# Two transformer blocks on one core: norm sums by quarters of tokens, context scaled early by GpSimd, attention scores a step ahead

## The chip, the cores and the metric

One core of one Trainium2 chip runs the whole kernel, in float32 results throughout. The metric is device time in microseconds (us) of one execution. PE is TensorE, PEld its weight loads, DVE is VectorE, ACT is ScalarE, POOL is GpSimd, SP is SyncE, which issues the loads.

## The reference, cut to what matters

There are 256 latent tokens and 256 context tokens of width 1024. A first block (state space mixer, pooling, gates, then a routed mixture of 32 experts) is followed by a second one of two layers: feed-forward, mixer, feed-forward; the mixer of layer 0 is gated linear attention beside latent attention, that of layer 1 is a neighbourhood attention. After each part stands a norm over the 1024 features of each token:

```python
def layer_norm_2(x):
    mu = jnp.mean(xf, axis=-1, keepdims=True)
    var = jnp.mean(jnp.square(xf - mu), axis=-1, keepdims=True)
    return ((xf - mu) * lax.rsqrt(var + EPS)).astype(x.dtype)
def modulate_2(x, shift, scale):
    return x * (1.0 + scale) + shift
xl = post_norm_2(xl, 0.5 * g1 * swiglu_2(modulate_2(xl, sh1, sc1), ffn1_w_in[l], ffn1_w_out[l]))
```

Layer norms: after the first block's mixer ("out1", latents, 256 columns) and after its experts ("out2", 256); then after feed-forward 1, mixer and feed-forward 2 of layer 0 and feed-forward 1 of layer 1 (512 columns, latents and context together), and after the mixer and feed-forward 2 of layer 1 (256 columns). RMS norms stand in the first block's gate (over 2048 features), in the gated linear attention (each of 4 heads, 128 features) and in the latent projections (128 and 384 features).

## The kernel before, in words

Activations lie transposed: 128 features on the partitions, tokens along the columns, 8 tiles for 1024 features. A linear layer multiplies with three fp32r products for each pair of tiles: weights and activations are each cut into a high part (ACT copies to fp32r, AH and HR) and a low part (DVE subtracts, AL and LR). Weights come in loads of up to 1 MB through three slots; ACT's and DVE's `take` cut a load two ahead of the one that PE uses. Each engine has its own program in its own order (`tensor_program`, `scalar_program`, `vector_program`, `pool_program`), tied by counting semaphores; all order around the change is written out by hand.

Sums over features are fp32 matmuls with `K.onesD`, a 128x128 matrix of 1/1024, so that every partition gets the sum of its column. `mean_pe` (L567) adds the tile m-1 to the mean after PE's linear tile m, so that seven of eight sums stand among the linear's matmuls, and the last follows the last residual (`residual_dve`). Then `norm_dve` (L625) subtracts the mean from the eight tiles, `norm_act` (L612) squares them, `norm_pe` (L600) sums the squares, ACT takes the root over all columns into `rs`, DVE inverts it there (`V.rec`, L259), and multiplies each tile. ACT scales and shifts a multiplied tile, cuts its high part, DVE its low part (`lead_act`, `lead_dve`), and PE's next linear starts with tile 0. POOL multiplies the residual (`lead_pool`).

```python
    S.wait_ge(*pe.of(tag, "var"))
    S.wait_ge(*act.last)
    S.act(rs, K.ps(tag, "var")[:, 0:n], ACT.Sqrt, bias=K.eps[:, eps:eps + 1]).then_inc(*act(tag, "root"))
```

Between the experts and the first feed-forward, `after_dve` (L2087) adds the residual, cuts eight tiles of the scaled context, cuts two loads of weights and only then centres; `after_act` (L2060) scales the context. The context's tokens are loaded to `K.X` while the experts run (`route_sp`). The gated linear attention ends with one RMS norm per head (`gla_pe` from L2334, `gla_act`, `gla_dve`), and `latent_pe` (L2687), `latent_act`, `latent_dve` begin with two more. In the neighbourhood attention (`odd_pe` L2928, `odd_act`, `odd_dve`) a step is one head and half of the queries, 32 steps. In step n PE issues the scores of n, then in every second step the values of an earlier head, then the transposes of n-2. DVE adds the bias, takes the maximum, and later multiplies by the inverse sum; ACT takes the exponential and copies transposes and values out of PSUM.

PSUM has eight banks in rotation (`Tensor.bank`); during a norm one is held for the mean and one for the variance. The conditioning steps (`conditioning_pe`) are 16 fp32 matmuls of a weight tile 128x32 (`K.CS`) with 128 columns, each to one of four groups of 32 output partitions; the trace counts each fp32 matmul as two instructions.

## Time and profile before

| | us |
|---|---|
| median of 3 runs | 3332.53 (3329.27 to 3336.29) |
| the profiled execution | 3333.78 |
| its span | 3332.0 |
| outside the span | 1.78 |
| PE busy | 3049.1 (92% of the span) |
| DVE busy | 1418.6 (43%) |
| ACT busy | 1079.1 (32%) |
| POOL busy | 308.4 (9%) |
| mean granted TensorE clock | 0.957 of full |

A share of busy time is an average over stages with different limits. A matmul's end is modelled, so its start and the start of the next tell what it takes. The experts ran in the branch "few", in which every expert has at most 64 tokens.

### The profile page before, as it was taken

Reading aid. Unit: us, or ns where it says so; the run is one execution under the profiler, and the core shown is the slowest. Engines: PE = TensorE matmul, PEld = TensorE weight load, DVE = VectorE, ACT = ScalarE, POOL = GpSimd, SP = SyncE. Lnnn points to the kernel's source line nnn. Section 1 sums busy time; section 2 is a strip of 40 time slices with the busy share of each in tenths; the row PEclk is TensorE's granted clock in tenths of the full one; section 3 lists DMA queues with packets and bytes.
Section 4 is the critical chain, followed back from the end, with each engine's and each line's share of the span. In section 5 each row is a group of like instructions: output and inputs, shape, how many; then the busy total and the mean of one; then the engine's idle time right before and its main releaser. Section 6 shows DMA issues by size and latency. Waiting matters only on the chain.

```text
span 3332.0 us, 43660 instructions
## 1 busy us (share of the span) xinstructions
PE 3049.1 (92%) x18814; PEld 2358.7 (71%) x18814; DVE 1418.6 (43%) x2096; ACT 1079.1 (32%) x1579; POOL 308.4 (9%) x309
## 2 busy tenths in 40 slices
PE   6988899789999979999887888999989999897998
PEld 4866699755555548888676546888768887773898
DVE  4654554532222243333576554333353333436554
ACT  4443453322222233222432233322242221434443
POOL 0024470100000000000104001000010000300000
PEclk9988999879999989999999899999999999999999
DMA  7556754489999943232339121333222323310363
GB/s 226 159 188 219 252 162 135 133 335 392 392 389 395 393 158 98 81 112 71 100 114 335 39 76 51 103 94 102 81 78 88 107 81 103 129 62 1 127 188 103
DMA packets 415213, 537.27 MB, mean 161 GB/s; under 512 B 14340, under 2 KB 389924, under 8 KB 390308
## 3 DMA queue, kind: packets, MB, share of 16 engines
q1 hardware_dynamic: 415012, 534.38, 47.0%
q8 instruction: 151, 2.47, 0.3%
q14 instruction: 50, 0.41, 0.0%
HBM read 533.30 MB, written 1.05 MB: 160 GB/s over the span
## 4 chain that ended last, share of the span: by engine, by line
PE 83%; DVE 8%; ACT 4%; DMA 2%; issue 2%; SPq 0%; POOL 0%; DVEq 0%; ACTq 0%; POOLq 0%
PE ps L188 80%; PE ps L187 2%; ACT ar L313 2%; DVE ar L243 2%; DVE LR L243 1%; DMA RAW<-in_ada_w 1%; DVE ar L259 1%; ACT HR L313 1%; PE ps L194 1%; DVE ar L249 0%; DVE ar L253 0%; DMA RAW<-in_w_in 0%; DVE ar L262 0%; ACT AH L313 0%; DVE X L243 0%
## 5 line engine op out<-in xcount | busy, mean ns | idle before, releaser
L188 PE MATMUL ps<-AH,HR 128*128 128x512 f32 (+1 forms) x2552 | 902.4, 354 | 64.1 <-DVE AL L243 40.5
L188 PE MATMUL ps<-AL,HR 128*128 128x512 f32 (+1 forms) x2552 | 888.6, 348 | 0.0
L188 PE MATMUL ps<-AH,LR 128*128 128x512 f32 (+1 forms) x2552 | 887.6, 348 | 0.0
L243 DVE TENSOR_TENSOR LR<-RAW,HR 128x2048 fp32r<-128x2048 f32 (+3 forms) x232 | 485.4, 2094 | 597.8 <-ACT HR L313 595.1
L313 ACT ACTIVATE HR<-RAW 128x2048 fp32r<-128x2048 f32 (+3 forms) x232 | 404.1, 1744 | 736.9 <-PE ps L188 634.9
L188 PEld LDWEIGHTS ps<-AH,HR 128*128 128x128 f32 x2552 | 492.1, 193 | 136.7 <-ACT arf1i L313 20.3
L188 PEld LDWEIGHTS ps<-AL,HR 128*128 128x128 f32 x2552 | 492.3, 193 | 59.8 <-issue 1.9
L188 PEld LDWEIGHTS ps<-AH,LR 128*128 128x128 f32 x2552 | 491.7, 193 | 58.9
L188 PE MATMUL ps<-ar 64*128 64x128 f32 (+9 forms) x1318 | 237.1, 370 | 59.4 <-ACT ar L313 26.8
L249 POOL TENSOR_SCALAR X<-X 128x512 f32<-128x512 f32 (+2 forms) x50 | 83.8, 1700 | 2220.2 <-ACT AH L313 1608.9
L188 PEld LDWEIGHTS ps<-ar 64*128 64x128 f32 (+2 forms) x1318 | 140.5, 189 | 139.1 <-issue 45.6
L253 DVE SCALAR_TENSOR_TENSOR X<-ps,mod,X 128x256 f32<-128x256 f32 x152 | 67.4, 480 | 284.9 <-PE ps L188 284.9
L243 POOL TENSOR_TENSOR ar<-ar 128x384 f32<-128x384 f32 (+5 forms) x138 | 151.9, 1109 | 291.0 <-DVE ar L243 116.3
L313 ACT ACTIVATE ar<-ar 128x384 f32<-128x384 f32 (+7 forms) x208 | 109.4, 557 | 158.8 <-DVE ar L249 53.9
L313 ACT ACTIVATE ar<-ps 128x256 f32<-128x256 f32 (+4 forms) x190 | 89.2, 475 | 203.8 <-PE ps L188 194.9
L188 PE MATMUL ps<-BHf1i,HR 128*128 128x512 f32 x352 | 144.5, 410 | 0.7 <-ACT arf1i L313 0.7
L188 PE MATMUL ps<-RAW,CS 128*32 128x128 f32 x3072 | 125.9, 315 | 16.6 <-DMA RAW<-in_w_ada 9.0
L313 ACT ACTIVATE ar_few<-ps 128x512 f32<-128x512 f32 x64 | 46.9, 733 | 287.4 <-PE ps L188 287.4
L188 PE MATMUL ps<-BHf1i,LR 128*128 128x512 f32 x352 | 139.7, 397 | 0.0
L188 PE MATMUL ps<-BLf1i,HR 128*128 128x512 f32 x352 | 139.6, 396 | 0.0
L188 PE MATMUL ps<-BHf2i,HR 128*128 128x512 f32 (+1 forms) x352 | 122.7, 349 | 1.4 <-DVE arf2i L243 1.4
L188 PE MATMUL ps<-BHf2i,LR 128*128 128x512 f32 (+1 forms) x352 | 119.1, 338 | 0.0
(182 smaller groups left out, 3748.8 us busy)
## 6 DMA issues: line engine op xcount, KB each, us to landing
RAW<-in_ada_w SPq DMA_DIRECT2D x72, 1024.0 KB, 6.4
RAW<-in_f1i SPq DMA_DIRECT2D x44, 1024.0 KB, 5.1
RAW<-in_f2i SPq DMA_DIRECT2D x44, 1024.0 KB, 5.1
RAW<-in_w_in SPq DMA_DIRECT2D x32, 1024.0 KB, 5.5
RAW<-in_w_ada SPq DMA_DIRECT2D x24, 1024.0 KB, 8.0
RAW<-in_w_eu SPq DMA_DIRECT2D x17, 1024.0 KB, 10.0
HF<-in_w_ed SPq DMA_DIRECT2D x17, 1024.0 KB, 7.5
LF<-in_w_eu SPq DMA_DIRECT2D x17, 1024.0 KB, 10.1
```

Source lines behind the costliest of these rows:

```text
L187: return self.e.matmul(o, w, x, start=start, stop=stop, skip_group_check=True)
L188: return self.e.matmul(o, w, x, start=start, stop=stop)
L194: return self.e.transpose(o, a, self.K.ident[sp:sp + q, sp:sp + q])
L243: return self.e.tensor_tensor(o, a, b, op) if self.e else NOTHING
L249: return self.e.tensor_scalar(o, a, s1, None, o1)
L253: return self.e.scalar_tensor_tensor(out=o, in0=a, scalar=s, in1=b, op0=o1, op1=o2) if self.e else NOTHING
L259: return self.e.reciprocal(x, x) if self.e else NOTHING
L313: return self.e.activation(o, a, f, **k) if self.e else NOTHING
```

## The change

A sum goes by quarters of the tokens: four matmuls with a 128x32 matrix of 1/1024, each for a quarter of the columns, each to its own 32 partitions, so that the sums take a quarter of the columns. ACT's and DVE's steps on sums are then on 64 or 128 columns instead of 256 or 512, and four matmuls with a matrix that picks a row spread the result to all partitions and columns in PSUM. The mean now needs this spreading too, with a copy by ACT ahead of it. The same is done for the RMS norms. `meanwhile` puts work between two steps of a norm. `T.bi = 7` lets the rotation go on with bank 0. In the neighbourhood attention PE issues the scores of step n+1 in step n, and ACT's order changes in odd steps. POOL sets the picking matrix `K.pick` (128x4x128) in `setup_pool` by five more fills. `latent_act` takes all four squares first, then both roots; `latent_dve` inverts both (128 columns), and `latent_pe` spreads both ahead of the projections. The diff, cut; the edits for `rs` in the calls of `norm_act` and `norm_dve` are left out.

```diff
+def sums_pe(T, K, b, x, n, first, last):
+    w = n // 4
+    for g in range(4):
+        r = T.mm(b[32 * g:32 * g + 32, 0:w], K.onesD[:, 0:32], x[:, g * w:(g + 1) * w], first, last)
+    return r
+def spread_pe(T, K, b, x, n):
+    w = n // 4
+    for g in range(4):
+        r = T.mm(b[:, g * w:(g + 1) * w], K.pick[:, g, :], x[:, 0:w], True, True)
+    return r
 def norm_pe(T, K, tag, n, sq):
-    vb, held = T.hold(6, tag, "var")
+    mb, held = T.hold(6, tag, "mean")
...
+    T.wait_ge(*act.of(tag, "mean row"))
+    spread_pe(T, K, mb, K.stat, n).then_inc(*pe(tag, "mean"))
+    vb, held = T.hold(7, tag, "var")
...
     for k in range(8):
-        T.wait_ge(*K.act.of(tag, "sq", k))
-        r = T.mm(vb[:, 0:n], K.onesD[:, :], sq[:, k, :], k == 0, k == 7)
+        T.wait_ge(*act.of(tag, "sq", k))
+        r = sums_pe(T, K, vb, sq[:, k, :], n, k == 0, k == 7)
+    r.then_inc(*pe(tag, "var"))
+    rb, held = T.hold(6, tag, "factor")
...
+    T.wait_ge(*dve.of(tag, "factor row"))
+    spread_pe(T, K, rb, K.stat, n).then_inc(*pe(tag, "factor"))
+    T.hi, T.bi = 8, 7
 def norm_act(S, K, tag, x, n, eps, sq, post, meanwhile=None):
+    row = K.stat[:, 0:n // 4]
+    S.wait_ge(*pe.of(tag, "sums"))
+    S.act(row, K.ps(tag, "sums")[:, 0:n // 4], ACT.Copy).then_inc(*act(tag, "mean row"))
+    K.free(act, tag, "sums")
+    if meanwhile:
+        meanwhile()
...
+    S.act(row, K.ps(tag, "var")[:, 0:n // 4], ACT.Sqrt, bias=K.eps[:, eps:eps + 1]).then_inc(*act(tag, "root"))
 def norm_dve(V, K, tag, x, n, pre, post, meanwhile=None):
+    if meanwhile:
+        meanwhile()
     V.wait_ge(*act.of(tag, "root"))
+    V.rec(K.stat[:, 0:n // 4]).then_inc(*dve(tag, "factor row"))
+    V.wait_ge(*pe.of(tag, "factor"))
...
-            V.tt(x[:, k, :], x[:, k, :], rs, MUL).then_inc(*dve(tag, "normed", k))
+            V.tt(x[:, k, :], x[:, k, :], K.ps(tag, "factor")[:, 0:n], MUL).then_inc(*dve(tag, "normed", k))
 def merge_pe(T, K):
...
-        T.mm(ssq[:, 0:256], K.onesD[:, :], o.sq[m % 2], m == 0, m == 15).then_inc(*pe("ssq", m))
+        sums_pe(T, K, ssq, o.sq[m % 2], 256, m == 0, m == 15).then_inc(*pe("ssq", m))
...
+    T.wait_ge(*dve.of("rz row"))
+    spread_pe(T, K, b, K.stat, 256).then_inc(*pe("rz"))
...
...
+    S.wait_ge(*pe.of("rz"))
+    S.act(o.rz, K.ps("rz")[:, 0:256], ACT.Copy).then_inc(*act("rz"))
+def context_pool(G, K):
+    m = K.mod2[0]
+    G.wait_ge(K.loaded["ctx2"], 16)
+    for k in range(8):
+        G.ts(K.route.h32[:, k, :], K.X[:, k, 0:256], m[:, 8 + k, 1:2], m[:, k, 1:2], MUL, ADD).then_inc(K.scaled, 1)
 def few_pool(G, K):
-    pass
+    context_pool(G, K)
 def after_act(S, K):
...
+    S.wait_ge(K.scaled, 8)
+    for k in range(8):
+        S.act(K.AH[:, k * 512:k * 512 + 256], o.h32[:, k, :], ACT.Copy).then_inc(*act("f1i0h", 1, k))
...
-    for k in range(8):
-        half(k, 0, 1, k % 2)
-    S.cut(1)
-    norm_act(S, K, "out2", o.XL, 256, 0, o.h32, o.rs, post)
+    norm_act(S, K, "out2", o.XL, 256, 0, o.sq2, post, lambda: S.cut(0))
 def after_dve(V, K):
...
-    for k in range(8):
-        half(k, 0, 1, k % 2)
-    V.cut(1)
+    def meanwhile():
+        for k in range(4, 8):
+            context(k)
+        V.cut(0)
+    for k in range(4):
+        context(k)
+    norm_dve(V, K, "out2", o.XL, 256, ("ln2g", "ln2b"), latents, meanwhile)
 def gla_pe(T, K):
...
+    def factor(hd):
+        T.wait_ge(*dve.of("ofactor row", hd))
+        spread_pe(T, K, bank("ofactor", hd), o.rss[hd], 512).then_inc(*pe("ofactor", hd))
...
-        T.mm(bank("omean", hd)[:, :], K.onesD[:, :], o.sqs[hd % 2], True, True).then_inc(*pe("omean", hd))
+        sums_pe(T, K, bank("omean", hd), o.sqs[hd % 2], 512, True, True).then_inc(*pe("omean", hd))
...
+        if hd:
+            factor(hd - 1)
+    factor(3)
 def gla_dve(V, K):
...
+    def onorm(hd):
+        V.wait_ge(*pe.of("ofactor", hd))
+        then(V.stt(o.oT[:, hd, :], o.oT[:, hd, :], K.v("gng"), K.ps("ofactor", hd)[:, :], MUL, MUL))
+        then(V.tt(o.oT[:, hd, :], o.oT[:, hd, :], o.r[:, hd, :], MUL))
...
-        then(V.rec(rs))
+        V.rec(o.rss[hd]).then_inc(*dve("ofactor row", hd))
...
+        if hd:
+            onorm(hd - 1)
+    onorm(3)
 def odd_pe(T, K):
...
+    scores(0)
     for n in range(36):
-        if n < 32:
-            hd, qt = n // 2, n % 2
-            p, m = 64 * (hd % 2), hd // 2
-            T.mm(bank("nsc", n)[:, :], o.qT[p:p + 64, m, qt * 128:qt * 128 + 128], o.kT[p:p + 64, m, :], True,
-                 True).then_inc(*pe("nsc", n))
+        if n < 31:
+            scores(n + 1)
 def odd_act(S, K):
...
     for n in range(36):
+        if n % 2 and 2 <= n < 34:
+            turned(n - 2)
         if n < 32:
+            share(n)
...
+        if n % 2 == 0 and 2 <= n < 34:
+            turned(n - 2)
```

## Rows read from the trace of the kernel before

**Rows 1.** The page: chain that ended last, by engine.
```profile
PE 83%; DVE 8%; ACT 4%; DMA 2%; issue 2%; SPq 0%; POOL 0%; DVEq 0%; ACTq 0%; POOLq 0%
```

**Rows 2.** Chain of waits after the first FFN: start us, us, what.
```profile
1616.83 1.14 PE ps L188 x2
...
1619.40 7.15 PE ps L188 x16
...
1626.57 0.70 ACT arf1i L313
...
1634.03 11.14 PE ps L188 x38
```

**Rows 3.** Timeline there: start, us, engine, line, op [idle before].
```profile
1599.94 1.02 PE L188 MATMUL ps<-X,onesD 128*128 128x512 f32 x2
...
1601.03 0.39 PE L188 MATMUL ps<-BLf1i,HR 128*128 128x512 f32 x1
...
1623.60 1.28 ACT L313 ACT_TABLE_LOAD   x1
```

**Rows 4.** Timeline, PE, a conditioning step among fp32r matmuls.
```profile
112.97 1.08 PE L188 MATMUL ps<-RAW,CS 128*32 128x128 f32 x32
...
114.33 0.40 PE L188 MATMUL ps<-AL,HR 128*128 128x512 f32 x1
114.57 0.40 PE L188 MATMUL ps<-AH,LR 128*128 128x512 f32 x1
```

**Rows 5.** Groups of DVE by form: reciprocals.
```profile
L259 DVE RECIPROCAL ar<-ar 128x512 f32<-128x512 f32 x11 | 36.9, 3353 | 16.3 <-ACT ar L313 16.1
...
L259 DVE RECIPROCAL ar<-ar 128x256 f32<-128x256 f32 x4 | 7.0, 1752 | 11.6 <-ACT ar L313 11.6
```

**Rows 6.** Groups of ACT by form: PSUM to SBUF, 128 columns.
```profile
L313 ACT ACTIVATE mrow<-ps 128x128 f32<-128x128 f32 x96 | 26.2, 273 | 112.7 <-PE ps L188 95.6 <-DMA X<-in_ctxT 16.9
```

**Rows 7.** Timeline, PE: latent projections; full 128x128 weights, 128 columns.
```profile
1906.09 1.91 PE L188 MATMUL ps<-ar,RAW 128*128 128x512 f32 x2
...
1909.88 1.05 PE L188 MATMUL ps<-RAW,ar 128*128 128x128 f32 x8
1910.77 1.02 PE L188 MATMUL ps<-ar,RAW 128*128 128x512 f32 x2
```

**Rows 8.** Windows: width, PE, PEld, DVE, ACT, POOL busy, granted clock, DMA.
```profile
1628.00:1630.00 2.00, 0.00 (x0) 0.00 (x0) 2.00 (x1) 0.00 (x0) 0.00 (x0) 0.64 0.00 0
...
1638.00:1640.00 2.00, 2.00 (x9) 1.60 (x8) 2.00 (x4) 1.97 (x5) 2.00 (x2) 0.80 0.00 0
```

**Rows 9.** Chain of waits, the last norm (256 columns).
```profile
3318.29 3.73 PE ps L188 x16
...
3324.34 0.43 DVE X L243
```

**Rows 10.** Timeline, DVE, POOL and PE, between the experts and the first FFN.
```profile
1219.10 0.75 DVE L243 TENSOR_TENSOR AL<-tmp,AH 128x256 fp32r<-128x256 f32 x2
...
1231.60 2.73 DVE L243 TENSOR_TENSOR X<-X,ps 128x256 f32<-128x256 f32 x8
...
1242.33 11.67 POOL L249 TENSOR_SCALAR X<-X 128x512 f32<-128x512 f32 x8 [572.20 <-DVE X L243]
...
1243.57 0.77 PE L188 MATMUL ps<-AH,HR 128*128 128x512 f32 x1 [5.60 <-DVE AL L243]
```

**Rows 11.** Chain of waits, end of the gated linear attention.
```profile
1884.07 0.69 ACT ar L313
...
1894.58 0.64 ACT ar L313
```

**Rows 12.** Waits in the neighbourhood attention: us in total, times, longest.
```profile
DVE ar L243 <- PE ps L188: 17.1, 9, 3.5
...
DVE AL L243 <- ACT AH L313: 14.5, 7, 3.2
```

**Rows 13.** Windows: eight steps of that attention.
```profile
2985.83:3013.32 27.49, 21.02 (x81) 9.76 (x81) 18.64 (x51) 13.17 (x30) 0.00 (x0) 1.00 0.00 0
```

More of the change, by code:

```diff
@@ L564, in row_ready @@
     return lambda k: [K.act.of(tag, "hi", k), K.dve.of(tag, "lo", k)]
+def sums_pe(T, K, b, x, n, first, last):
[8 more added lines that the diff above has]
+    return r
 def mean_pe(T, K, tag, x, n, bank=7):
     T.hi = 7
-    mb, held = T.hold(bank, tag, "mean")
+    mb, held = T.hold(bank, tag, "sums")
     for h in held:
@@ L575, in add @@
         T.wait_ge(*K.dve.of(tag, "x", m))
-        r = T.mm(mb[:, 0:n], K.onesD[:, :], x[:, m, :], m == 0, m == 7)
+        r = sums_pe(T, K, mb, x[:, m, :], n, m == 0, m == 7)
         if m == 7:
-            r.then_inc(*K.pe(tag, "mean"))
+            r.then_inc(*K.pe(tag, "sums"))
     def after(m):
@@ L617, in norm_act @@
     S.wait_ge(*pe.of(tag, "var"))
-    S.wait_ge(*act.last)
-    S.act(rs, K.ps(tag, "var")[:, 0:n], ACT.Sqrt, bias=K.eps[:, eps:eps + 1]).then_inc(*act(tag, "root"))
+    S.act(row, K.ps(tag, "var")[:, 0:n // 4], ACT.Sqrt, bias=K.eps[:, eps:eps + 1]).then_inc(*act(tag, "root"))
     K.free(act, tag, "var")
@@ L765, in setup_pool @@
 def setup_pool(G, K):
-    for t, v in ((K.onesD[:, :], 1.0 / 1024), (K.ones[:, :], 1.0), (K.eps[:, 0:1], 1e-5), (K.eps[:, 1:2], 1e-6)):
+    for t, v in ((K.onesD[:, :], 1.0 / 1024), (K.ones[:, :], 1.0), (K.eps[:, 0:1], 1e-5), (K.eps[:, 1:2], 1e-6),
+                 (K.pick[:, :, :], 0.0)):
         G.fill(t, v).then_inc(*K.pool("constants"))
+    G.wait_ge(*K.pool.last)
+    for g in range(4):
+        G.fill(K.pick[32 * g:32 * g + 1, g, :], 1.0).then_inc(*K.pool("constants"))
+        G.wait_ge(*K.pool.last)
 def setup_act(S, K):
@@ L1214, in merge_pe @@
     pe.note("h1 read")
+    b, held = T.bank("rz")
+    for w in held:
+        T.wait_ge(*w)
+    T.wait_ge(*dve.of("rz row"))
+    spread_pe(T, K, b, K.stat, 256).then_inc(*pe("rz"))
     linear_pe(T, K, "ya", "w_branch_a", None, 16, 0, 8, o.yv, 256,
@@ L1257, in merge_act @@
     S.wait_ge(*pe.of("ssq", 15))
-    S.act(o.rz, K.ps("ssq")[:, 0:256], ACT.Sqrt, bias=K.eps[:, 0:1], scale=0.5).then_inc(*act("rz"))
+    S.act(K.stat[:, 0:64], K.ps("ssq")[:, 0:64], ACT.Sqrt, bias=K.eps[:, 0:1], scale=0.5).then_inc(*act("rz root"))
     K.free(act, "ssq")
@@ L1298, in merge_dve @@
         V.tt(o.xsL[:, m, :], o.xsL[:, m, :], o.sil[m % 2], MUL).then_inc(*dve("yz", m))
-    V.wait_ge(*act.of("rz"))
-    V.rec(o.rz).then_inc(*dve("rz"))
+    V.wait_ge(*act.of("rz root"))
+    V.rec(K.stat[:, 0:64]).then_inc(*dve("rz row"))
     for m in tiles(V, 8, 16):
@@ L2041, in few_pool @@
 def few_pool(G, K):
-    pass
+    context_pool(G, K)
 def after_pe(T, K):
@@ L2700, in latent_pe, with factor @@
             T.wait_ge(*act.of("csq", i, m))
-            T.mm(b[:, :], K.onesD[:, :], o.P[1], m == 0, m == nt - 1).then_inc(*pe("cmean", i, m))
+            r = sums_pe(T, K, b, o.v2[:, i + m, :], 512, m == 0, m == nt - 1)
+        r.then_inc(*pe("cmean", i))
+    def factor(i):
+        b = bank("cfactor", i)
+        T.wait_ge(*dve.of("cfactor row", i))
+        spread_pe(T, K, b, o.P[0][:, 128 * i:128 * i + 128], 512).then_inc(*pe("cfactor", i))
+    factor(0)
+    factor(1)
     j, w = T.weights("ukv", None, 0, 1, 0, 1024, False)
@@ L2762, in latent_act @@
     meet(S, K, "gla end")
[L2763 to L2764 removed]
+    for i, (x, nt) in enumerate(((o.ck, 1), (o.cq, 3))):
         for m in range(nt):
[L2766 to L2773 removed]
+            S.act(o.v2[:, i + m, :], x[:, m, :], ACT.Square).then_inc(*act("csq", i, m))
+    for i, w in enumerate((8.0, 1024.0 / 384)):
+        S.wait_ge(*pe.of("cmean", i))
+        S.act(o.P[0][:, 128 * i:128 * i + 128], K.ps("cmean", i)[:, 0:128], ACT.Sqrt, bias=K.eps[:, 1:2],
+              scale=w).then_inc(*act("croot", i))
         K.free(act, "cmean", i)
@@ L2829, in then @@
         V.wait_ge(*dve.last)
+    for i in range(2):
+        V.wait_ge(*act.of("croot", i))
+        then(V.rec(o.P[0][:, 128 * i:128 * i + 128]), "cfactor row", i)
     for i, (x, nt, key) in enumerate(((o.ck, 1, "kvng"), (o.cq, 3, "qng"))):
-        V.wait_ge(*act.of("croot", i))
-        then(V.rec(o.P[0]))
+        V.wait_ge(*pe.of("cfactor", i))
         for m in range(nt):
-            then(V.stt(x[:, m, :], x[:, m, :], K.v(key, m), o.P[0], MUL, MUL), "cnorm", i)
+            then(V.stt(x[:, m, :], x[:, m, :], K.v(key, m), K.ps("cfactor", i)[:, :], MUL, MUL), "cnorm", i)
+        K.free(dve, "cfactor", i)
     V.take()
```

142 lines of the change are left out of this document (71 added, 71 removed).

## The prediction

> **What bounds the kernel now.** I read the page first: PE holds 83% of the chain that ended last, DVE and ACT 12% [rows 1]. So a change can pay in two ways: fewer columns in a stretch where PE never waits, or a shorter handover where PE does. I then took the chain and the timeline of one norm with 512 columns [rows 2, 3], a conditioning step, which is the same instruction shape as the new sums [rows 4], groups for the durations of small operations [rows 5, 6, 7], the granted clock [rows 8], and the places that the change touches by itself: the last norm [rows 9], the stage before the first feed-forward [rows 10], the end of the gated linear attention [rows 11], the neighbourhood attention [rows 12, 13]. The sum is made against the profiled execution (3333.78 us, span 3332.0 and 1.78 outside it); the median is 1.25 lower. A difference under 0.2%, 6.7 us, I count as none.
>
> **Sums inside the linears.** Two fp32 instructions with onesD and 512 columns start at 1599.94, and the second product behind them at 1601.03; less one product of 0.24 the sum takes 0.85 [rows 3, 4]. Four sets of four quarter matmuls with 128 columns start at 112.97, and the second product behind them at 114.33: 1.12 for four sets and the change back to full weights [rows 4]. With r for a set and c for the change of shape, 4r + c = 1.12: a lone set costs r + c, 0.28 if c is 0, 0.66 if c is 0.5. I take 0.36 (c = 0.1), because neither step of the row stands out. A sum with 256 columns is half of 0.85, 0.43; its set has half the columns and the same instructions; bounds 0.15 and 0.5, and I take 0.30. In each linear six sums are wholly inside PE's stream (the seventh ends while DVE does the last residual): 4 norms x 6 x 0.49 = 11.8, 3 x 6 x 0.13 = 2.3. The 16 sums over z give 2.1, of which I count 1.1 since PE has small waits there; the spreading and the copy of rz (0.9 + 0.4) stand between the last gate and the first product with yv, and cost about 0.8. **-14.4.**
>
> The row shows that a group in the quartered shape takes 1.0 us for 16 matmuls, about a quarter of 16 x 0.22, which full matmuls with as many columns take [rows 7]. Beside it the Trainium skill (TensorEngine Tiling (Array Packing), Key Properties) says that changing the tiling mode, not just the tile, drains TensorE. By that rule c would be paid at each of the 24 + 34 lone sums; at c = 0.5 the 58 sums would give back 0.3 each, 17 us, and the time would be 3295; the row's 1.12 for four sets with one change leaves room for that, but not for more.
>
> **The norm with 512 columns, four times.** Now, from the last residual to PE's next linear (1616.83 to 1634.03) it is 17.2 [rows 2]. Term by term:
> - Mean: before, 1.14 + 0.03. Now the last set 0.5 with its tail, ACT's copy of 128 columns 0.27 [rows 6], the spreading. Four full matmuls with 128 columns take 1910.77 - 1909.88 = 0.89 [rows 7], and 0.2 for the tail; 1.1. With four handovers 2.0. **+0.8.**
> - Squares to root: PE's squares are slower than ACT's: ACT is through at 1623.5, PE at 1626.55 [rows 2, 3]. With sets of 0.36 PE keeps up, and ACT's table load comes due, 1.28 from 1623.60 [rows 3]: the root starts at 1624.9 instead of 1626.57. **-1.7.**
> - Root on 128 columns: nearest is the copy, 0.27; with a bias 0.37 against 0.70. **-0.3.**
> - Reciprocal: 3.35 for 512 and 1.75 for 256, that is 6.25 ns a column and 0.15 fixed, so 0.95 for 128 [rows 5]. **-2.4.**
> - Spreading the factor, new: 1.1 at full clock. But PE has been idle some 2.3 us by then; in this stage the granted clock fell from 1.0 to 0.5 within 4 us after PE's last matmul, and was back at 1638 to 1640, 4 to 6 us after it started [rows 8]. At half clock it is 2.0. I take **+1.5**.
> DVE's multiplication from PSUM costs what it did (0.7), and ACT's scaling paces the next tiles as before. A norm gains 2.1 (bounds 1.1 and 3.0): **-8.4** for four.
>
> **The norm with 256 columns, three times** (out1, nout, the last). Mean +1.1 (the same number of instructions, full weights). PE's squares end at 3322.0 [rows 9], with ACT's table load just before it: -0.1. Root -0.25. Reciprocal 0.55 against 1.75: -1.2. Spreading +1.1 to +2.0. Net +0.65 to +1.55, so **+3.3** for three: these lose on the handover and win it back in the stream.
>
> **Before the first feed-forward.** DVE cuts the context from 1219.10, then two loads of weights, and centres only from 1231.60; PE starts at 1243.57 [rows 10]. Now GpSimd, idle for 572 us before 1242.33 [rows 10], scales the context while the experts run: eight operations with half the columns of those at 1242.33, under 1.5 us each, hidden by PE's work on the experts; without that cover they would cost up to 12. DVE's work ahead of centring is four subtractions (1.4), to 1220.6, and the spread mean is there at 1220.9: centring starts 10.7 earlier. Squares, table load and root are through at 1226.3, but DVE has four subtractions and one cut of weights (2.3) between, to 1227.2; reciprocal and spreading to 1228.8, and PE at 1232.0: -11.6. The second load is cut later now: ACT waits for POOL's last multiplication (11.67 long, from 1230.8), cuts it by 1244.4, DVE by 1246.8; PE wants it at 1245.9. +0.9. **-10.7** (bounds -7 and -13).
>
> **Gated linear attention and latents.** The last head's roots and reciprocals are 1884.07 to 1894.58 [rows 11]: reciprocal, two steps, twice over. With reciprocals of 0.95 and the spreading of head n under the norm of head n-1, DVE is done at 1890.0: -4.5. Then four squares in a row (2.3) in place of four rounds with PE, both roots, both reciprocals, two spreadings at half clock, one norm: PE's projections start at about 1897 instead of 1906.09 [rows 7], -9.0, and run longer at half clock, 4 us where it was 1.7: +1.2. **-7.8** (bounds -5 and -10).
>
> **Scores a step ahead.** Eight steps take 27.49 us, 3.44 each; DVE is busy 2.33 of it and PE 2.63 [rows 13]. DVE stands 17.1 us over all steps for the scores, which PE issues behind values and transposes [rows 12]; with the scores of n+1 issued a step early, that wait goes. Next late is the low part of every second pair, for which DVE waits on ACT (14.5 now [rows 12]); ACT is in turn behind an exponential. Following DVE, ACT and PE in their new orders through four steps gives 9.7 of DVE's work with its handovers and 1.7 of waiting for that low part: 11.4 where it is 13.74 now, 2.34 x 8 = 18.7. I take the smaller, the wait itself: **-17** (bounds: 0 if the other wait takes its place, -26 if PE's 2.63 a step binds alone).
>
> **At nothing.** The five fills at the start end long before the first weights have landed. Beginning with bank 0 only keeps PE off banks 6 and 7: the factor's bank is read until the eighth tile is multiplied, some 12 us, and the rotation comes to it later; without it PE would wait that long.
>
> **Sum.** -14.4 - 8.4 + 3.3 - 10.7 - 7.8 - 17 = -55.0: 3333.8 becomes 3278.8, and by the median 3277.5.
>
> **Rivals.**
> - The attention gains little, because the low part's wait takes over: 3277.5 + 15 = 3292.5. For it: that wait is nearly as long. Against: in its new order ACT reaches the values no later. Chance 0.13.
> - It gains more: DVE's own work binds the attention, PE's clock stays full through shorter gaps (0.9 less at each spreading): 3277.5 - 9 - 7 = 3261.5. Chance 0.10.
> - Slower: a quarter sum by itself, between full matmuls, does not run its four parts side by side, as they do in a row of sixteen, and pays for both changes of shape. Then a set takes 8 x 0.11 and about 0.3, 1.2. Against the forecast the linears lose 24 x 0.84 = 20 (512 columns) and 34 x 0.9 = 31 (256); the squares wait for PE again, 8 x 1.2 = 9.6 where the table load leaves 5.5 and 3.6: 4 x 4.1 + 4 x 6.0 = 40. The time is 3277.5 + 91 = 3368; it decides from a set of about 0.9, where the 55 us are used up. Against: 1.12 for sixteen matmuls [rows 4]. Chance 0.04. (It is the drain of the page above, at its worst.)
> - The clock stays at half after each sparser norm for so long that it takes the rest: 55 us lost are 110 us at half clock. Against: 4 to 6 us per norm now [rows 8]. Part of it gives a time within 0.2% of before, chance 0.02.
>
> **How the numbers follow.** The forecast has 0.71, and 3277.5 is its time; the bounds of its terms, taken as independent, are 12 us to either side. For 8 in 10 the range reaches to the times of the first two rivals and a little past them: 3257 to 3297. Faster: 0.94; the same: 0.02; slower: 0.04.
>
> **What would show it.** 128x32 matmuls on X in the linears at 0.3 to 0.4 a set; PE's gap after the first feed-forward near 15 us; the reciprocal of 128 columns at 0.95; centring of out2 near 1221 on the old scale; DVE's wait for scores near zero, and the 32 steps in about 93 us instead of 110. I am wrong if a lone set takes over 0.8, if the attention's pair of steps stays at 6.9, or if the clock after a norm stays at 0.5 for over 8 us.

## The result and the profile after

The changed kernel takes **3296.49 us** (median of 4 runs, 3292.12 to 3300.18) where the kernel before took 3331.03 beside it (4 runs, 3329.27 to 3336.29). The ratio is 0.9893, with a 95% interval of 0.9880 to 0.9905: faster by 34.5 us by the medians. The forecast was 55 us faster, 3277.5; the measured time lies half a microsecond inside the upper end of its range (3257 to 3297). The profiled execution took 3299.07 us, with a span of 3297.3.

The page of the changed kernel (busy times, then the chain that ended last by engine; it answers to [rows 1]):

```profile
PE 3044.2 (92%) x19910; PEld 2357.8 (72%) x19910; DVE 1381.8 (42%) x2096; ACT 1072.3 (33%) x1580; POOL 317.3 (10%) x322
...
PE 82%; DVE 8%; ACT 5%; DMA 3%; issue 2%; POOL 1%; SPq 0%; DVEq 0%; ACTq 0%; POOLq 0%
```

PE is busy 5 us less and the span is 35 us shorter, so 30 us of PE's idle time have gone. That doesn't make the gain all waiting: the mean granted clock fell from 0.957 to 0.949, and laid over the clock's records PE's busy time holds 252 us at half clock where it held 201. Counted at full clock PE's work shrank by some 30 us, and half clock took about 26 of it back. To see where the gain came, I cut both traces at the starts of GpSimd's multiplications of the residual, which begin when the first tile of the next linear is ready, right after each norm. The timeline of POOL after (start us, us, line, op):

```profile
1233.93 11.69 POOL L249 TENSOR_SCALAR X<-X 128x512 f32<-128x512 f32 x8 [536.32 <-ACT AH L313]
1621.80 13.45 POOL L249 TENSOR_SCALAR X<-X 128x512 f32<-128x512 f32 x8 [376.18 <-ACT AH L313]
...
2049.11 13.44 POOL L249 TENSOR_SCALAR X<-X 128x512 f32<-128x512 f32 x8 [235.96 <-ACT AH L313]
2434.17 13.44 POOL L249 TENSOR_SCALAR X<-X 128x512 f32<-128x512 f32 x8 [371.62 <-ACT AH L313]
2819.25 13.43 POOL L249 TENSOR_SCALAR X<-X 128x512 f32<-128x512 f32 x8 [371.63 <-ACT AH L313]
...
3085.37 7.58 POOL L249 TENSOR_SCALAR X<-X 128x256 f32<-128x256 f32 x8 [222.25 <-ACT AH L313]
```

| stretch | before, us | after, us | difference | forecast |
|---|---|---|---|---|
| up to the norm before the first FFN | 1242.33 | 1233.93 | -8.4 | -10.7 |
| first FFN and its norm | 391.01 | 387.87 | -3.1 | -5.0 |
| linear attention, latent attention, norm | 433.11 | 427.31 | -5.8 | -12.8 |
| second FFN, norm | 390.74 | 385.06 | -5.7 | -5.0 |
| third FFN, norm | 388.63 | 385.08 | -3.6 | -5.0 |
| neighbourhood attention, norm | 276.36 | 266.12 | -10.2 | -16.7 |
| last FFN, norm, store | 209.82 | 211.93 | +2.1 | +0.3 |

(The forecast column is the terms of the prediction put into their stretches.) All seven have the forecast's sign, and six of them came out worse.

Two rows need care. The first depends on the execution: the join, where the engines' programs meet behind the experts' branch (PE's row `ones,ident` marks it), is at 1215.6 in the trace before, and at 1211.2 and 1210.7 in the traces of experiments 1 and 8, which have the same code up to there. Only what lies behind the join can be read to better than some 5 us: PE's next linear starts 27.95 behind it before (27.8 and 29.2 in experiments 1 and 8) and 20.7 after (20.5 in experiment 7), so -7.2. The second FFN's extra 2 us have no counterpart in the third, which is the same code. In the kernel before PE waits once in the second FFN and not in the third:

```profile
2378.11 0.50 PE L188 MATMUL ps<-BHf2i,HR 128*128 128x512 f32 x1 [1.41 <-DVE arf2i L243]
```

That wait of 1.41 us is in all three traces with the FFN's code of before and in none of the nine with the changed one. Which edit removed it no run shows; no term of the forecast has it.

**A norm with 512 columns.** The chain of waits after the first FFN (start us, us, what), beside [rows 2]:

```profile
1606.58 0.04 issue
1606.63 0.47 PE ps L188 x8
...
1607.12 0.29 ACT stat L313
...
1607.45 1.17 PE ps L188 x8
...
1609.37 4.81 ACT arf1i L313 x8
...
1614.20 1.28 ACT L313
...
1615.49 0.38 ACT stat L313
...
1615.89 0.96 DVE stat L259
...
1616.99 2.06 PE ps L188 x8
...
1622.49 3.75 PE ps L188 x8
```

From the end of the last residual (1606.58) to PE's next linear (1622.49) it is 15.9 where it was 17.2. The mean costs 2.07 up to the centring (1608.65) where it cost 1.21; ACT's root now follows its table load without a wait for PE and starts 8.9 behind the residual instead of 9.8; root and reciprocal are 0.38 and 0.96. What is new is the spreading of the factor: 2.06, at half clock. The granted clock is at half from 1609.5 to 1626.6, 17 us, where before it was from 1628.6 to 1638.8, 10 us: it now falls at the first squares, behind PE's idle time on both sides of the mean's spreading. Most of the longer stretch lies in PE's waits; the next linear has 4.1 us of it (4.8 before).

**A lone sum in the stream**, by PE's timeline there (start us, modelled us), beside [rows 3]:

```profile
1597.70 0.40 PE L188 MATMUL ps<-BHf1i,LR 128*128 128x512 f32 x1
1598.03 0.43 PE L188 MATMUL ps<-X,onesD 128*32 128x128 f32 x8
1598.38 0.50 PE L188 MATMUL ps<-BHf1i,HR 128*128 128x512 f32 x1
1598.72 0.40 PE L188 MATMUL ps<-BLf1i,HR 128*128 128x512 f32 x1
```

Products follow each other by 0.234 us. From the product ahead of the set to the second one behind it there are 1.02 us: 0.55 for the set. The full sum cost 0.85 by the same reading. There is a step of 0.33 ahead of the set and one of 0.34 behind it, each 0.1 more than a product's, as if both changes of shape were to be seen. The change between fp32r products and fp32 sums goes with them, but costs nothing by itself: a full-shape sum between the same products takes 0.85 [rows 3], and one in before's row of squares 0.86 (1620.36 to 1621.22).

**Before the first feed-forward** (timeline of PE, then of DVE; beside [rows 10]; the join, the sums, the start of centring, then the second load of weights):

```profile
1214.47 0.30 PE L188 MATMUL ps<-ones,ident 128*128 128x32 f32 x2
1217.79 1.94 PE L188 MATMUL ps<-X,onesD 128*32 128x64 f32 x64 [3.02 <-DVE X L253]
1220.07 0.48 PE L188 MATMUL ps<-stat,pick 128*128 128x64 f32 x1 [0.34 <-ACT stat L313]
1221.16 1.75 PE L188 MATMUL ps<-stat,pick 128*128 128x64 f32 x7 [0.61 <-issue]
...
1235.17 0.76 PE L188 MATMUL ps<-AH,HR 128*128 128x512 f32 x1 [3.38 <-DVE AL L243]
...
1250.31 0.47 PE L188 MATMUL ps<-AH,HR 128*128 128x512 f32 x1 [1.29 <-DVE LR L243]
```

```profile
1214.81 3.23 DVE L253 SCALAR_TENSOR_TENSOR X<-ps,mod,X 128x256 f32<-128x256 f32 x8 [2.46 <-PE ps L188]
...
1222.95 2.74 DVE L243 TENSOR_TENSOR X<-X,ps 128x256 f32<-128x256 f32 x8 [3.58 <-PE ps L188]
...
1247.87 6.70 DVE L243 TENSOR_TENSOR LR<-RAW,HR 128x2048 fp32r<-128x2048 f32 x3 [3.96 <-ACT HR L313]
```

Centring starts 8.5 us behind the join (16.0 before). PE's sums start 3.0 behind DVE's first residual (1.2 before), and one of the spreading's eight matmuls is followed by 0.61 of "issue", in which PE waits for nothing in the profile. The granted clock is at half from 1217.0 to 1240.9, so the sums, both spreadings and the first 5.7 us of the linear run at half clock. GpSimd's multiplications end at 1245.6, only then do ACT and DVE cut the second load, and PE waits 1.29 for it.

**Neighbourhood attention**: DVE's waits over its steps (us in total, times, longest), beside [rows 12]:

```profile
DVE AL L243 <- ACT AH L313: 10.8, 6, 1.8
DVE ar L243 <- PE ps L188: 8.6, 1, 8.6
DVE ar L243 <- PE ps L194: 8.0, 4, 3.1
```

The wait of 8.6 is the one ahead of the first scores; the kernel before has the same one (8.62, outside the window of [rows 12]). The waits for scores inside the steps went from 17.1 to 8.0, in four places, not to zero; those for the low part from 14.5 to 10.8. Between two low parts (four steps) there are 11.78 us, where there were 13.74 [rows 13]; but the group around 2981 takes 14.4 and two others 12.9. PE's timeline tells the two kinds apart (values and scores of two steps, at full and at half clock; over the two rows themselves the granted clock is 1.00 and 0.51):

```profile
2968.15 2.99 PE L188 MATMUL ps<-ar 64*128 64x512 f32 x10
...
2974.78 5.63 PE L188 MATMUL ps<-ar 64*128 64x512 f32 x10
```

**End of the linear attention and the latents**, chain of waits and PE's timeline, beside [rows 7, 11]:

```profile
1874.74 0.38 ACT ar L313
...
1881.25 2.45 ACT ar L313 x5
```

```profile
1888.40 1.53 PE L188 MATMUL ps<-ar,RAW 128*128 128x512 f32 x2
```

The last head's roots begin 1874.74, ACT's squares of the latents 1881.25, 6.5 us later (10.5 before); PE's projections begin at 1888.40, 13.7 behind the roots' start (22.0 before).

### The profile page after: what moved, and what is told of

Same layout as the page of the kernel before. It is cut to its first block, busy times and chain, and to the rows that moved or that the text cites. A ratio compares the mean times of both kernels' runs of the same rounds, so it can differ in the third digit from the quotient of the medians.

```text
span 3297.3 us, 45861 instructions
## 1 busy us (share of the span) xinstructions
PE 3044.2 (92%) x19910; PEld 2357.8 (72%) x19910; DVE 1381.8 (42%) x2096; ACT 1072.3 (33%) x1580; POOL 317.3 (10%) x322
## 4 chain that ended last, share of the span: by engine, by line
PE 82%; DVE 8%; ACT 5%; DMA 3%; issue 2%; POOL 1%; SPq 0%; DVEq 0%; ACTq 0%; POOLq 0%
PE ps L188 79%; DVE ar L243 2%; PE ps L187 2%; ACT ar L313 2%; DMA RAW<-in_ada_w 1%; DVE LR L243 1%; ACT HR L313 1%; DVE ar L259 1%; DVE ar L249 1%; DMA RAW<-in_w_in 1%; PE ps L194 1%; ACT arf1i L313 1%; DVE ar L262 1%; ACT L313 1%; DVE ar L253 1%
## 5 line engine op out<-in xcount | busy, mean ns | idle before, releaser
L313 ACT ACTIVATE ar<-ps 128x512 f32<-128x512 f32 (+4 forms) x191 | 89.4, 476 | 216.8 <-PE ps L188 194.7
```

Of the source, the lines that this page charges most:

```text
L313: return self.e.activation(o, a, f, **k) if self.e else NOTHING
```

## The experiments

Ten runs were made. Each was timed beside the kernel before; the ratio's interval is 0.1 to 0.2% to either side, 3 to 7 us, so the small effects are read from the stretches of the traces, and the totals only say that they add up.

**1. Scores a step ahead, alone.** The kernel before with the changed loops of the attention on PE and ACT, nothing else:

```diff
+    scores(0)
     for n in range(36):
-        if n < 32:
-            ...
+        if n < 31:
+            scores(n + 1)
```

> The kernel before with one part of the change only: in the neighbourhood attention the scores of step n+1 are issued during step n, and ScalarE takes its copies and exponentials in the new order. Theory A, from the trace after: at full clock four steps take 11.8 us instead of 13.74, six such groups give 11.8, and the stretches at half clock take a part of it back, so the whole kernel is 8 to 12 us shorter (3319 to 3323), with DVE waiting for scores only where the granted clock is below 1. Theory B, the forecast's: -17 (3314) and no such wait left. Theory C: the gain of about 11 in the trace after came from something else before it in time, then under 5 us here.

Measured: 3318.25, ratio 0.9958 (0.9944 to 0.9971), -14 us by the ratio; the stretch of the attention takes 262.68 instead of 276.36, -13.7. DVE's waits in it:

```profile
DVE ar L243 <- PE ps L194: 6.7, 5, 2.1
```

It lies between A and B, nearer to A's mechanism: waits of 1.16 us (four times) and 2.09 remain, each in or right behind a stretch in which the granted clock is at half. The part's gain is real and its own; theory C falls.

**2. Grouped sums.** The changed kernel, with the sums of six tiles in one row:

```diff
     def after(m):
-        if m:
-            add(m - 1)
+        if m == 6:
+            for i in range(6):
+                add(i)
         if m == 7:
+            add(6)
             add(7)
```

> The changed kernel, but the sums of the first six residual tiles are issued in one row behind the seventh tile's products, instead of one set behind each product. Theory A: a lone set costs r + c with c, the two changes of shape, about 0.36 us and r 0.19 (512 columns) or 0.09 (256), since 4r + c = 1.12 and the lone sets of the trace after cost 0.55 and 0.45. Then five changes go in each of seven linears: 7 x 5 x 0.36 = 12.6 us, 3284. Theory B: c is 0.1 as the forecast had it and a lone set costs more for another reason (its wait for DVE's residual, which a group has as well): 3.5 us, 3293. Theory C: the six tiles' sums behind each other make the last tile's products late for DVE: no gain.

Measured: 3277.45, ratio 0.9831 (0.9817 to 0.9845), which is 0.6% below the changed kernel. PE's timeline of one such row:

```profile
1591.11 0.39 PE L188 MATMUL ps<-BHf1i,LR 128*128 128x512 f32 x1
1591.43 1.52 PE L188 MATMUL ps<-X,onesD 128*32 128x128 f32 x48
1592.87 0.50 PE L188 MATMUL ps<-BHf1i,HR 128*128 128x512 f32 x1
1593.21 0.40 PE L188 MATMUL ps<-BLf1i,HR 128*128 128x512 f32 x1
```

1591.11 to 1593.21 is 2.10, less two products 1.63 for six sets: 6r + c = 1.63 and r + c = 0.55 give r = 0.22 and **c = 0.34**. With 256 columns the row takes 1.01 and the lone set 0.45: r = 0.11, c again 0.34. The first and the third FFN's stretches are 1.8 and 1.7 us shorter (386.12 and 383.40), five times 0.34; the second is only 1.0 shorter. A is right: the seven linears owe it 7 x 1.7 = 12 us. The total gained more (20, and the interval of that difference is about 6 us wide to either side). Part of the rest is a second effect of the row, which no theory has. In the linear ahead of the norm out1 the first lone set comes before DVE's first residual is there (timeline of PE, the changed kernel):

```profile
625.09 0.44 PE L188 MATMUL ps<-X,onesD 128*32 128x64 f32 x8 [1.30 <-DVE X L253]
```

PE waits, and the granted clock is at half from 623 to 630. With the row it neither waits nor loses the clock there: from this linear's start to PE's work behind its norm it is 31.0 us in both traces with grouped sums (experiments 2 and 6), and 36.3 and 35.7 in the two of the changed kernel, 4.7 less at least. The stretch with the latent attention gave 5.6, but it differs by 3.0 between two executions of the changed kernel.

**3. The mean by full weights in the norms with 256 columns**, squares still by quarters:

```diff
+        if n == 256:
+            r = T.mm(mb[:, 0:n], K.ones[:, 128:256], x[:, m, :], m == 0, m == 7)
+        else:
+            r = sums_pe(T, K, mb, x[:, m, :], n, m == 0, m == 7)
```

> The changed kernel, but in the four norms with 256 columns the mean is summed with full weights as before the change (two instructions a tile, no copy of a row, no spreading); the squares are still summed in quarters. Theory A: the copy and the spreading of the mean are what these norms lost at the handover, 1.1 to 1.5 each, and the lone sets of 256 columns bring nothing in the stream (0.45 against 0.43): 3 x 1.3 = 4 us, and before the first feed-forward PE has 16 instructions instead of 64 and 8 of spreading between the join and the centring, which then starts 2 to 3 us sooner: 6 to 7 in all, 3290. Theory B: the quarter sets pay in the stream as the forecast had it (0.13 each, 18 of them, 2.3): a gain of 1 to 2 for the three norms. Theory C: before the first feed-forward the late centring comes from the copy's wait, not from the number of instructions: centring 1.0 to 1.5 sooner.

Measured: 3288.03, ratio 0.9864 (0.9849 to 0.9878). The last FFN is 0.8 shorter, the attention with its norm 1.1, the stretch up to the first FFN 3.2, of which centring, 5.5 us behind the join instead of 8.5, is 3.0. The size is A's for the place before the first FFN and less than A's elsewhere. A's reason for that place, the number of PE's instructions, did not hold (experiment 6). The rest of the total is the latent attention again, 7.4 us shorter in this trace, at full clock early (experiment 7).

**4. Idle work in the norms.** Matmuls of constants into the bank that is overwritten next:

```diff
+def keep_pe(T, K, b, count):
+    for _ in range(count):
+        T.mm(b[:, 0:256], K.ident[:, :], K.ones[:, :], True, True)
...
+    keep_pe(T, K, rb, 5)
     T.wait_ge(*dve.of(tag, "factor row"))
     spread_pe(T, K, rb, K.stat, n).then_inc(*pe(tag, "factor"))
```

> The changed kernel with idle work for PE in every norm: matmuls of constants (128 x 256 columns, fp32) whose results are overwritten, three ahead of the first squares, five ahead of the spreading of the factor, seven behind it. They do nothing but occupy PE where it waits for DVE and ACT. Theory A: the granted clock fell in these waits (1.0 to 0.5 at 1609.8 in the trace after, 1.4 us of idle behind the first spreading) and costs the spreading 0.9 and the first 4 us of the next linear 2; kept at full, each of the eight norms gives back 2 to 3 us: 3275 to 3282. Theory B: the clock falls all the same, and the idle work is then at half clock, 6 us where 3.4 are free: each norm 2 to 3 us longer, 3315 to 3320. Theory C: the clock stays but the linear starts when its first operand is cut, so only the spreading's 0.9 comes: 3289.

Measured: 3291.69, ratio 0.9866 (0.9850 to 0.9882): against the changed kernel 5 us less by the medians, 9 by the ratios, 3 by the traces. The norm after the first FFN on PE's timeline (the idle work is the rows with ones,ident):

```profile
1617.28 2.43 PE L188 MATMUL ps<-ones,ident 128*128 128x256 f32 x10
1619.59 1.16 PE L188 MATMUL ps<-stat,pick 128*128 128x128 f32 x8
1620.58 3.19 PE L188 MATMUL ps<-ones,ident 128*128 128x256 f32 x14
1624.20 0.47 PE L188 MATMUL ps<-AH,HR 128*128 128x512 f32 x1 [0.43 <-DVE AL L243]
...
1625.85 0.47 PE L188 MATMUL ps<-AH,HR 128*128 128x512 f32 x1
```

The windows show a granted clock of 1.00 through this norm, and the spreading takes 1.16 instead of 2.05, its full-clock length. But from the last set of the mean to the next linear it is 14.9 us instead of 15.9, no more. ACT and DVE make a tile ready every 1.65 us (1624.20 to 1625.85), PE at full clock needs 1.40 for it (six products), so what PE loses at half clock on the first tiles it can mostly catch up by the eighth. That is nearest to theory C. The stretches bear it out: second and third FFN, attention and last FFN are 0.1, 1.0, 1.9 and 1.5 us shorter; the first FFN is 1.7 longer, where PE now waits 3.5 us for the second load of weights, which is cut behind GpSimd's end (1.29 in the changed kernel).

**5. Idle work in the attentions**: three matmuls ahead of every fourth transpose, five ahead of the latents' sums, twelve at the rotated keys.

```diff
         if 2 <= n < 34:
+            b = bank("npt", n - 2)
+            if n % 4 == 3:
+                keep_pe(T, K, b, 3)
             T.wait_ge(*dve.of("nshare", n - 2))
```

> The changed kernel with idle work for PE (matmuls of constants, results overwritten) outside the norms: three 256-column matmuls ahead of every fourth transpose of the neighbourhood attention, five ahead of the latents' sums, twelve where PE waits for the rotated keys in the latent attention. Theory A: in the attention the clock falls every 25 us behind a wait of PE, each fall makes DVE wait 1.15 or 2.6 to 3.1 us for the scores (8.0 in all in the trace after), and in the latent attention it stayed at half for 20 us instead of 6. Kept at full, the attention's group of four steps is 11.8 throughout (the marks around it 6 us closer) and the latent stage 3 to 8 shorter: 3283 to 3288. Theory B: the idle work delays the transposes by as much as it keeps: same as the changed kernel, 3296, with DVE's waits still there. Theory C: the clock falls at those points whatever PE does: 3300.

Measured: 3291.37 (3282.76 to 3299.98), ratio 0.9888 (0.9868 to 0.9908). Its profiled execution, with a span of 3281.0, is the fastest of the five. DVE's waits in the neighbourhood attention:

```profile
DVE AL L243 <- ACT AH L313: 12.7, 7, 1.8
...
DVE ar L243 <- PE ps L194: 1.8, 2, 1.1
```

But for one fall around 2940 the granted clock stays at 1.00 through its steps, every group of four takes 11.8, and the stretch takes 258.39 instead of 266.12: -7.7. In the latent attention the clock was at half for 7 us instead of 27, and that stretch took 420.14 instead of 427.31. Theory A, by this trace. The median does not show it: the interval of its ratio holds the changed kernel's 0.9893, and the mean granted clock of the four other executions is 0.952 to 0.957 where the profiled one has 0.958. So that the clock is kept each time isn't shown by this run; experiment 10 has the attention's part again (255.14).

**6. Three edits together**: grouped sums, the mean before the first FFN by full weights, and the second load cut ahead of GpSimd's end (`S.cut(1)` and `V.cut(1)` behind the last tile there).

> The changed kernel with grouped sums, the mean before the first feed-forward by full weights, and the second load of weights cut there by ACT and DVE right behind their last tile, no longer behind GpSimd's last multiplication. Against the grouped sums alone (3277.5): centring 5.5 us behind the join instead of 6.9 (-1.5); the second load is cut at about 1243.5 + 1.9 + 2.3 = 1247.7 on the scale of the trace after, instead of 1250.17, and PE, which wanted it at 1249.0, does not wait (-1.3): 3274 to 3276. Rival: DVE's cut of that load is pulled ahead of nothing, PE then waits later for the third load: -1.5 only, 3276.

Measured: 3283.17, ratio 0.9852 (0.9834 to 0.9871), 3277.0 to 3285.3: not below the grouped sums alone, so the expectation failed in the total. One half of it held: the first FFN's stretch takes 382.84 instead of 386.12, PE no longer waits for the second load. The other did not: the stretch ahead of it is 4.4 longer than with the grouped sums alone, of which 2.9 lie ahead of the join and 1.5 behind it, and the stretch with the latent attention is 2.5 longer. PE's sums ahead of centring, here and then in experiment 3, where the same 16 instructions stand:

```profile
1218.20 5.41 PE L188 MATMUL ps<-X,ones 128*128 128x256 f32 x16 [2.76 <-DVE X L253]
```

```profile
1216.10 3.72 PE L188 MATMUL ps<-X,ones 128*128 128x256 f32 x16 [1.43 <-DVE X L253]
```

In both, DVE's first residual starts 0.34 behind the join. The sums start 2.72 behind that residual here and 1.39 there; in the kernel before it was 1.17. Here they also run in part at half clock (0.68 over them), there at full. Nor is it where they lie in the order of PE's program: experiment 5 has the changed kernel's code up to there, and its sums start 1.38 behind the residual where the changed kernel's start 2.98. In these windows the DMA engines carry single packets of the queues of kind "instruction" and nothing else, and the pause behind the first spreading is booked as "issue"; a late arrival of PE's own code would look like that, but no run here shows it. The cause stays open.

**7. The changed kernel again.**

> The changed kernel once more, unaltered, to tell what of its trace is the kernel and what the execution. Theory A: the 20 us at half clock in the latent attention (6 us in the kernel before) and the late start of PE behind the join (3.0 after DVE's first residual where other kernels have 1.2 to 1.6) belong to the single execution: one or both are different this time, and the stage from the first feed-forward's norm to the next one takes 420 to 428. Theory B: they belong to the program as compiled (where the activity falls, where its instructions lie in memory): both are the same again, 427 and 3.0. The time is 3293 to 3299 either way.

Measured: 3293.47, ratio 0.9881 (0.9865 to 0.9897). The late start is there again (2.73 behind the first residual, and 0.61 of "issue" in the same place), as theory B has it. So is the long stretch at half clock in the latent attention, 27 us in both; the 3 us between the two executions (424.35 and 427.30) lie ahead of the latent projections. Over all traces: 27 us in six of the seven with the changed latents and no idle work there, 10 in the seventh (experiment 3, whose code in that stretch is the same), 10, 10 and 17 in the three with the latents of before, which are the same code there. So it goes with the change more often than not, and it is not fixed by the program. Its cost is read from the projections' start to the end of the stretch: 160.7 and 160.4 us with the 27 us and 155.0 with the 10, so 5 to 6 us. The windows of the changed kernel (us, PE busy, PEld, DVE, ACT, POOL, granted clock, DMA):

```profile
1931.00:1937.00 6.00, 5.98 (x11) 2.26 (x12) 3.70 (x7) 1.57 (x4) 0.00 (x0) 0.50 1.07 344
1937.00:1943.00 6.00, 6.00 (x13) 2.59 (x12) 2.63 (x9) 1.72 (x5) 0.00 (x0) 0.50 0.57 180
```

**8. Idle work in the kernel before's attention**, three matmuls where PE waits for ACT ahead of the values.

> The kernel before with idle work for PE in the neighbourhood attention only: three matmuls of constants (256 columns) where PE waits 1.3 to 1.5 us for ScalarE's copy ahead of the values, every second step. Theory A: the idle work fills PE's wait, the clock stays full, and what the two falls of the trace before cost (a wait for scores of 3.51 instead of 1.93, and the slow first steps) comes back: the stage 2 to 4 us shorter, and no more, since its group of four steps stays 13.74: 3328. So most of what idle work gives the changed kernel comes from its busier PE. Theory B: 3 x 0.42 just misses the wait's end, and every second step is later by it: 3335 to 3345. Theory C: the falls cost before as much as after: 7 us, 3324.

Measured: 3331.86, ratio 0.9999 (0.9991 to 1.0008). The attention's stretch is 2.5 us shorter, as theory A has it, and the latent attention's 6.4 longer in that trace (17 us at half clock where it had 10); the total shows nothing. DVE's regular wait for scores stayed, at 2.03 us where it was 1.93: it came from the order in which PE issued them, not from the clock, so before the change the idle work had little to win back.

**9. Without the rotation's start at bank 0** (`T.hi, T.bi = 8, 7` became `T.hi = 8`).

> The changed kernel without one line: the rotation of PSUM banks goes on behind a norm where the linear ahead of it left off, and does not begin with bank 0. The forecast says that PE would then wait for the bank of the factor, which DVE reads until its eighth multiplication, up to 12 us, wherever the next linear takes bank 6 among its first: at one or more of the seven norms that are followed by a linear, so 3305 to 3370. Rival: the rotation does not come to bank 6 so early: 3296, no difference.

Measured: 3310.33, ratio 0.9936 (0.9918 to 0.9954). PE's first product of the next linear, at the two norms where it shows:

```profile
1243.88 0.79 PE L188 MATMUL ps<-AH,HR 128*128 128x512 f32 x1 [9.44 <-DVE X L243]
```

```profile
3095.26 0.58 PE L188 MATMUL ps<-AH,HR 128*128 128x256 f32 x1 [6.22 <-DVE X L243]
```

PE waits for DVE's last multiplication, 9.44 us (3.38 in the changed kernel, for its first operand) and 6.22. The stretches that begin there are 4.1 and 4.7 longer, 9 us. The one up to the first FFN is 2.6 longer as well, but PE is already 3.8 us later at the start of out1's linear, ahead of the first norm with the edit; no other stretch is longer. The medians differ by 14. Two norms of seven show the wait.

**10. All that helped**: experiment 6 with the idle work of 4 (three, four, six) and 5.

> The combined kernel with the idle work of both earlier kinds (three, four and six matmuls in a norm; attention and latents as there). If the gains add: 3275 less 1 per norm for eight norms less what the attention and the latents gain (6 and 3 to 5): 3257 to 3262. If the clock is the same budget however it is spent (idle work in one place makes it fall in another), 3270 to 3275.

Measured: **3264.14**, ratio 0.9796 (0.9777 to 0.9815), below both kernels and below the grouped sums. The total is within 2 us of what was expected, but that sum started from 3275 for experiment 6, which measured 3283.17: the idle work gave 19 us here, where the expectation's parts make 17 to 19. By the traces it gave 3 (experiment 4) and 16 (experiment 5), so there the gains add. The mean granted clock of its span is 0.973 (0.949 after).

## Why the prediction was right in sign and large in size

- **Sums inside the linears** (forecast -14.4). The step that went wrong is "I take 0.36 (c = 0.1), because neither step of the row stands out". The row of sixteen [rows 4] was read from its first matmul on, which leaves out the change of shape ahead of it, 0.1 by the lone set's step; with it 4r + c is 1.22, which fits the r and c of experiment 2 (4 x 0.22 + 0.34), and a lone set is 0.55. The row alone could not split the two terms: one equation, and c was chosen. The 24 sums of 512 columns gave 24 x 0.30 = 7.2 and not 11.8; those of 256 cost 0.45 against 0.43 and gave nothing instead of 2.3, and the sums over z with the spreading of rz cost 0.2 (PE's start on the linear behind them) instead of giving 0.3. 8 us short. The page of the Trainium skill that stood against the change (TensorEngine Tiling (Array Packing), Key Properties: changing the mode drains TensorE) was the better guide to this term than the row as I read it; it gives no number, the runs give 0.34 us for both changes. The rival built on it (a set above 0.9) is far away. The 3295 that the prediction works out for c = 0.5 is nearly the measured time, but by luck: c is 0.34, and the sums explain 8 of the 20 us that are missing.
- **The norm with 512 columns** (-2.1 each). Mean, root and reciprocal came as forecast: +0.9 for 0.8, root 0.9 earlier for 0.9, reciprocal 0.96 for 0.95. The spreading of the factor costs 2.3 with its handovers where I took 1.5, between a full-clock and a half-clock price: the text itself had 2.0 for half clock and the row for it [rows 8]. So -1.3 each, 3 us short over four.
- **The norm with 256 columns** (+1.1 each). The same spreading at half clock: 1.96 in the last norm. Each handover is longer by 1.4 (out1, with its linear, where executions of the same code differ by as much), 1.7 and 1.7 (from the last residual to PE's next linear, or to the end). 1.5 us short.
- **Before the first FFN** (-10.7, bounds -7 and -13). GpSimd's work on the context was hidden, as forecast. But PE starts 20.7 us behind the join where it was 27.95, -7.2 for the -11.6 of the text, and with the wait for the second load -6.0: outside the bounds. PE's sums came late behind the join, which no row of before told of, and centring with them by 3 us; from centring to PE's start it is 12.2 us instead of 11.1, with the spreading at half clock. The second load of weights came later than forecast (1250.2, and PE wanted it at 1249.0): that wait was named, with 0.9 against 1.3. 5 us short; why the sums came late stays open. The stretch's -8.4 looks better by what differs ahead of the join.
- **Linear attention and latents** (-7.8). PE's projections start 13.7 us behind the last head's roots and not 22.0: 8.4, where the forecast had 9.0 and 1.2 of it given back at half clock. Mechanism and size held. Around it 5 us were lost that no term has. 2.2 of them went ahead of the roots (from the multiplication of the residual to the last head's roots 252.9 us, 250.7 before); the second execution of the changed kernel has 250.2 there, so they belong to the execution. The rest went behind the projections' start, in code that the change does not touch, where the clock stayed at half for 27 us (experiment 7).
- **Scores a step ahead** (-17). The step "with the scores of n+1 issued a step early, that wait goes" failed for about half: it went from 17.1 to 8.0. With PE at full clock a group of four steps takes 11.78 (forecast 11.4); where the clock falls, PE's values and scores take 5.63 us instead of 2.99, longer than DVE's own work, and PE is the late one. I had walked DVE, ACT and PE through four steps with PE's durations at full clock. Experiment 5 shows that cause: at full clock the waits inside the steps are 1.8 us in all and the stretch gains 7.7 more. With the norm's 1.7 taken out, the attention gave 12 us for 17: 5 short.
- **At nothing.** The fills and the bank rotation cost nothing; the rotation's line is worth 9 to 14 us, at two norms, less than the 12 a norm that the text allowed. But the changed kernel also lost the wait of 1.41 us in the second FFN, for a PSUM bank by its releaser, which the forecast had not seen.
- **The rivals.** "The attention gains little" gave nearly the right time (3292.5) by luck: the low part's wait did not take over, it fell too. "It gains more, as the clock stays full" did not happen by itself; experiment 10 had to pay for the clock with idle work. Of the signs of being wrong, a lone set is 0.55 (not over 0.8) and a pair of attention steps 5.9 (not 6.9). The clock behind a norm stays at half for 17 us in all, over the 8 of the text, though only 4.1 us of it lie in the next linear.

Together the terms are some 27 us short: 8 + 3 + 1.5 + 5 + 5 (linear attention and latents) + 5 (neighbourhood attention). 7 came from elsewhere: 2.5 in the second FFN, 1.3 in the first, 0.4 in the third, and some 3 ahead of the join, where executions of the same code differ by more. That leaves the 20 that are missing. The time fell inside the range partly by that luck; the mechanisms named were right, and what was sized wrong was c, the clock at which PE's part of each handover and of the attention runs, and the start behind the join.

## What to carry to other kernels

A quarter-shaped matmul group pays for its change of shape once, so put such groups side by side: one row of six instead of six lone ones was worth 12 us, more than quartering the sums had been (7). The row also moves the first sum away from an operand that isn't there yet. Price a term on PE at the clock its stretch is granted, and once an engine's waits have been taken away ask what the next one does at half clock. Where PE is waited for and itself waits a microsecond or two ahead of that, matmuls of constants in that wait are cheap and can be worth more than the tuning around them (7.7 us in the attention's trace); where another engine paces the work they give little (about 1 us a norm).

Two traces of the same code differed here by up to 5 us in one stretch: read an effect between two marks close to it, as the join and the next linear, and not from a stretch's length.

## What was not expected of the hardware

- A change between full and quarter weight shape cost 0.34 us for there and back, at 128 and at 64 columns alike; the change between fp32r and fp32 in the full shape cost nothing that the starts show (0.85 us for a lone sum, 0.86 in a row).
- Behind the join, PE's first sums came 1.2 to 1.7 us behind DVE's first residual in eight traces and 2.7 to 3.1 in four; two with the same instructions there had 1.39 and 2.72, and two executions of the changed kernel 2.98 and 2.73.
- In the neighbourhood attention the granted clock fell to half four times up to the last scores once they were issued early (at 2944, 2975, 3002 and 3026), three times in the kernel before (2970, 3021 and 3028), and once with the short idle work in PE's waits (2938).
- In the latent attention PE worked without a gap from 1925.0 to 1947.4 at half clock (experiment 7 shows two windows of it), where the shortest of the other traces has 7 us at half in all and experiment 3, with the same code there, 10.
